# Down weights of the experts issued from ScalarE's queue behind its eviction of the results, gate and up weights left on SyncE's queue

## The reference, cut to what matters

```python
def hier_moe(x, w_group, w_expert, w_gate, w_up, w_down):
    ...
    hid = jax.nn.silu(lax.ragged_dot(xs, w_gate, sizes)) * lax.ragged_dot(xs, w_up, sizes)
    ys = lax.ragged_dot(hid, w_down, sizes) * weight.reshape(-1)[order][:, None].astype(x.dtype)
    return jax.ops.segment_sum(ys, tok_sorted, num_segments=n_tok).reshape(b, s, d)
```

## Time and profile before

| | us |
|---|---|
| median of 3 runs | 3278.77 (3275.36 to 3280.22) |
| the profiled execution | 3283.96 |
| its span, first to last instruction | 3282.1 |
| first expert stage, first gate matmul to last down matmul | 331.0 to 816.4 |
| second expert stage, the same | 1242.6 to 1728.0 |

### The profile page before, as it was taken

How to read it: one execution, slowest core, us unless ns; L and a number is a source line. 1 busy time by engine, 2 the same in 40 slices (tenths; PEclk the granted TensorE clock), 3 DMA queues, 4 the chain that set the end, 5 groups by cost and what they waited for, 6 DMA issues and landing times. The chain is left out here.

```text
span 3282.1 us, 37064 instructions
## 1 busy us (share of the span) xinstructions
PE 2668.1 (81%) x13270; PEld 1813.9 (55%) x13270; DVE 1187.2 (36%) x2020; ACT 789.8 (24%) x1304; POOL 225.7 (7%) x313
## 2 busy tenths in 40 slices
PE   8885998877488868988882986799996987599997
PEld 4534665444234445654441763577785763477776
DVE  2544110000345441100005745455533744455532
ACT  0320010000035300100001225244421325244421
POOL 0001111111000001111110000000001000000000
PEclk9997999999699978999996998899998999799999
DMA  3043999998410348999993300222222210222221
GB/s 119 1 188 136 365 406 409 409 406 331 133 26 1 143 180 322 403 408 409 411 372 113 103 26 13 90 90 89 89 90 70 93 39 13 77 90 89 89 90 64
DMA packets 189581, 573.97 MB, mean 175 GB/s; under 512 B 40656, under 2 KB 119952, under 8 KB 140082
## 3 DMA queue, kind: packets, MB, share of 16 engines
q1 hardware_dynamic: 178930, 555.97, 44.5%
q0 software_dynamic: 10560, 16.81, 1.6%
HBM read 567.47 MB, written 23.07 MB: 180 GB/s over the span
## 5 line engine op out<-in xcount | busy, mean ns | idle before, releaser
L1281 PE MATMUL ps<-layer_h_hi,layer_w_hi 128*128 128x512 f32 x1024 | 406.2, 397 | 49.2 <-issue 23.6
L1283 PE MATMUL ps<-layer_h_hi,layer_w_lo 128*128 128x512 f32 x1024 | 399.8, 390 | 0.0
L1282 PE MATMUL ps<-layer_h_lo,layer_w_hi 128*128 128x512 f32 x1024 | 399.3, 390 | 0.0
L859 PE MATMUL ps<-w_weights,moe_xsT 128*64 128x256 f32 x2688 | 313.8, 381 | 55.6 <-DMA w_weights<-in_moe_w_up 35.3
L914 DVE TENSOR_TENSOR moe_hid<-moe_silu,ps 128x256 f32<-128x256 f32 x64 | 27.0, 421 | 796.7 <-PE ps L859 796.7
L859 PEld LDWEIGHTS ps<-w_weights,moe_xsT 128*64 128x64 f32 x2688 | 223.2, 137 | 155.9 <-issue 107.1
L1281 PEld LDWEIGHTS ps<-layer_h_hi,layer_w_hi 128*128 128x128 f32 x1024 | 192.6, 188 | 112.3 <-issue 70.1
L1332 DVE TENSOR_TENSOR layer_w_lo<-layer_raw,layer_w_hi 128x2048 fp32r<-128x2048 f32 x52 | 119.2, 2292 | 279.7 <-ACT layer_w_hi L1328 279.7
L1283 PEld LDWEIGHTS ps<-layer_h_hi,layer_w_lo 128*128 128x128 f32 x1024 | 192.6, 188 | 41.2
L1282 PEld LDWEIGHTS ps<-layer_h_lo,layer_w_hi 128*128 128x128 f32 x1024 | 192.8, 188 | 38.9 <-issue 0.8
L877 PE MATMUL ps<-w_weights,moe_hidT 128*64 128x512 f32 x672 | 180.6, 685 | 38.5 <-DVE moe_hidT L916 38.5
(11 more groups left out here) (350 smaller groups left out, 3853.2 us busy)
## 6 DMA issues: line engine op xcount, KB each, us to landing
w_weights<-in_moe_w_gate SPq DMA_DIRECT2D x84, 1024.0 KB, 28.2
w_weights<-in_moe_w_up SPq DMA_DIRECT2D x84, 1024.0 KB, 29.1
w_weights<-in_moe_w_down SPq DMA_DIRECT2D x84, 1024.0 KB, 28.9
first_ring<-in_moe_w_gate SPq DMA_DIRECT2D x44, 1024.0 KB, 28.2
first_ring<-in_moe_w_up SPq DMA_DIRECT2D x44, 1024.0 KB, 29.1
first_ring<-in_moe_w_down SPq DMA_DIRECT2D x44, 1024.0 KB, 29.0
layer_raw<-in_ffn_up SPq DMA_DIRECT2D x44, 1024.0 KB, 5.1
layer_raw<-in_w_in SPq DMA_DIRECT2D x24, 1024.0 KB, 5.1
```

The source lines that it names most:

```text
L859: ins = pe.matmul(k.ps[64 * h:64 * h + 64, 2 + m, 0:256], xsT[:, j, :], weights.gate_up[s][m][:, j, 256 * h:256 * h + 256], start=j == 0, ...
L1281: pe.matmul(out, stationary[0], moving[0], start=first, stop=False)
L1282: pe.matmul(out, stationary[0], moving[1], start=False, stop=False)
L1283: return pe.matmul(out, stationary[1], moving[0], start=False, stop=last)
```

## The change

SyncE no longer issues the down weights in the loops over the first 31 blocks. ScalarE does: after it has copied the result of block b to `ys`, it issues the two down chunks of expert b+3, with no wait of their own, because it has already waited for `used[s][5]`. The gate and up weights stay on SyncE's queue, and so do all six chunks of the first three experts and of the last loop.

```diff
-    def load(self, sp, s, e, before):
+    def load(self, sp, s, e, before, with_down=True):
...
+        if with_down:
+            self.load_down(sp, s, e, before)
+
+    def load_down(self, eng, s, e, before):
+
+        a = self.k.a
         for c in range(2):
             before(4 + c)
-            sp.dma_start(self.down[s][:, 2 * c:2 * c + 2, :].rearrange("p j c -> p (j c)"),
+            eng.dma_start(self.down[s][:, 2 * c:2 * c + 2, :].rearrange("p j c -> p (j c)"),
                          a["moe_w_down"][self.layer, e, c * 256:(c + 1) * 256, :].rearrange("(p j) c -> p (j c)", j=2)).then_inc(self.loaded[s][4 + c], 16)
...
             with sp.Fori(1, TURNS) as i:
                 for s in range(WEIGHT_SETS):
-                    weights.load(sp, s, i * WEIGHT_SETS + s, free(s, i))
+                    weights.load(sp, s, i * WEIGHT_SETS + s, free(s, i), with_down=False)
             for s in range(LAST_SET):
-                weights.load(sp, s, TURNS * WEIGHT_SETS + s, free(s, TURNS))
+                weights.load(sp, s, TURNS * WEIGHT_SETS + s, free(s, TURNS), with_down=False)
...
-            for_each_block(act, n, body)
+            def body_and_load(s, times, b):
+                body(s, times, b)
+                weights.load_down(act, s, b + WEIGHT_SETS, lambda c: None)
+
+            with act.Fori(0, TURNS - 1) as i:
+                for s in range(WEIGHT_SETS):
+                    body_and_load(s, i, i * WEIGHT_SETS + s)
+            for s in range(WEIGHT_SETS):
+                (body_and_load if s < LAST_SET else body)(s, TURNS - 1, (TURNS - 1) * WEIGHT_SETS + s)
+            for s in range(LAST_SET):
+                body(s, TURNS, TURNS * WEIGHT_SETS + s)
+            with act.Fori(0, n) as q:
+                body(LAST_SET, q + TURNS, q + (EXPERTS - 1))
```

## The result

The changed kernel takes 3294.85 us (median of 5 runs, 3289.14 to 3296.95), the kernel before 3275.97 beside it (5 runs, 3274.73 to 3280.22). The ratio is 1.0053, 95% interval 1.0038 to 1.0067: 12 to 22 us slower, about 17 (the two medians are 18.9 us apart). The forecast was +9. The time lies inside the wide range, 3273 to 3304, that had to cover the rivals too; it lies just above the 3281 to 3294 of the forecast itself, and +17 is above the +3 to +14 of its mechanism. The profiled execution has a span of 3295.1 us, 13.0 more than before.

What follows compares the result with a forecast made beforehand. DMA transfers of weights were taken to bound the expert stages. Zero terms plus tail growth of 3.7 and 5.2 us gave 8.9, taken as 9: 3278.77 + 9 = 3287.8 us; forecast's own range 3281 to 3294, wide range 3273 to 3304.

Steps and rivals of the forecast that it cites:

- Issue time: On SyncE: taking two load issues of six from it gains nothing, 0 us.
- ScalarE's hold: On ScalarE: two more issues behind each copy, about 0.9 us, fit in before silu is needed, 0 us.
- start of the loads: Down loads issued after the copy start slightly later; DMA engines still have queued work, 0 us.
- The order in which chunks are served: DMA queues take turns; down chunks overtake gate and up chunks, landing in about 9.8 us; the part with a price.
- T: Landing of a stage's last weight chunk, set by the sum of transfers; expected within 2 us of 811.8 in the first stage.
- Gate loads "still some 28" us: Sign expected in the profile: gate loads on SyncE's queue still land some 28 us after issue.
- The tail, +3.7 and +5.2: TensorE's end behind the last landing grows to 8.3 us, by 3.7 in the first expert stage and 5.2 in the second.
- so block 30 starts at T - 19.2: Stage end: block 29's last up chunk lands at T - 27.2, and block 30's first matmul follows 8.0 us later.
- Nothing moves: Rival: second queue served behind the first, or TensorE's lead at the end as before; -3 to +3 us, chance 0.20.
- Starvation: Rival: ScalarE's queue gets under a third of the turns, down chunks come late; 3306 us, chance 0.06.
- Disturbance: Rival: two queues slow each other's transfers, up to 210 us (3490); any size above 0.1 us per block, chance 0.07.
- Faster: Rival: three queues taking turns halve the gather's collision cost, 22 us off and 9 added; 3266 us, chance 0.11.

Runs made afterwards that it cites:

- run after the next silu: Changed kernel, but ScalarE issues the two down loads behind the next block's silu instead of behind the copy: 3296.57 us, ratio 1.0051 to the kernel before.
- run with one row: Kernel before, with ScalarE issuing two extra loads of one 16-byte row per block into an unused tile: 3281.25 us, ratio 1.0011.
- one chunk: Changed kernel, but ScalarE issues only chunk 5 of each expert and chunk 4 stays on SyncE: 3283.3 us, ratio 1.0018 to the kernel before.
- every second: Kernel before, with ScalarE issuing chunks 1, 3 and 5 of experts 3 to 30 and SyncE chunks 0, 2 and 4: 3282.11 us, ratio 1.0019.
- halved kernel before: Kernel before with half of the gate and up matmuls left out, all loads and copies kept: 3268.93 us, ratio 0.9977 to the full kernel before.

## Why the prediction was right, and where it was off

*Issue time 0, ScalarE's hold 0, start of the loads 0*: right. ScalarE's timeline around a pair of issues:

```profile
594.14 0.60 ACT L901 ACTIVATE moe_ys<-ps 128x512 f32<-128x512 f32 x1 [9.24 <-PE ps L883]
594.30 0.83 ACTq L756 DMA_DIRECT2D w_weights<-in_moe_w_down  x2
595.45 1.28 ACT L898 ACT_TABLE_LOAD   x1 [0.71 <-issue]
597.53 0.38 ACT L898 ACTIVATE moe_silu<-ps 128x256 f32<-128x256 f32 x1 [0.80 <-PE ps L865]
```

The pair takes 0.83 us, and silu still waits 0.80 us for TensorE behind the table.

*The order in which chunks are served*: right in kind, too short in time. Down loads land 9.7 us (first) and 14.5 us (second) after issue; 9.7 us is four times 2.46, the time that I gave to the pair, but only the first chunk has landed by then: the pair takes half as long again as I had it. Each queue does get about half the turns (the 1.52 and 1.51 MB above), but not from the start: in the first 5 us after an issue ScalarE's queue moves 0.39 MB and SyncE's 1.45. First waits come at block 10, before block 15. The copies to `ys` come every 16.0 us in the middle:

```profile
L901 ACT ACTIVATE moe_ys<-ps x20: 597/597/597, 488.4 to 792.2; 128x512 f32<-128x512 f32 x20
```

(792.2 - 488.4)/19 = 15.99 us, with blocks 28 to 29 already at TensorE's pace. T is later by 1.1 and 0.7 us, within the 2 us allowed, and the last three blocks wait for nothing.

*Gate loads "still some 28" us*: wrong, in the second execution of the changed kernel, where the trace pairs them, they take 33 to 47, with a median of 41. SyncE is still held (a median of 1.9 us for a gate issue in the middle of the first stage, as before), so I take its queue to hold as many chunks as before, some eleven; in the middle of the stage it has only four sixths of the transfers, and 28.2 x 6/4 = 42 us. It changed nothing in the sum, because the count at the end goes by the order of landing and not by latency.

*The tail, +3.7 and +5.2*: the mechanism was right and the term too small; it measured +6.8 per stage. The count back from T was good: block 29's last up chunk landed at 782.07, T - 27.4 (predicted T - 27.2). The step that failed is the one that follows, "so block 30 starts at T - 19.2": block 30 no longer started from that landing. TensorE was at its own pace from block 29 on, one block earlier. Block 28's last up chunk landed at 767.54, T - 41.9, and from there to block 29's first matmul it took 778.88 - 767.54 = 11.3 us, not the 8.0 of the earlier trace rows. After the wait of 2.77 us the up matmuls took 3.60 instead of 1.95 us and the down matmuls 5.35 instead of 3.65: 3.35 us, all of the difference. The granted clock says why: it is at the lower level from 767.6 to 771.1 us and again from 774.5 to 777.9, and at the upper level between and behind. The last stretches of the changed kernel:

```profile
741.00:779.00 38.00, 32.37 (x197) 18.80 (x195) 2.88 (x6) 1.96 (x4) 4.95 (x10) 0.87 1.02 404
779.00:792.00 13.00, 12.06 (x94) 8.10 (x92) 1.44 (x3) 0.98 (x2) 2.37 (x4) 1.00 1.01 407
```

and the same part of the stage before:

```profile
741.00:783.00 42.00, 33.00 (x228) 19.98 (x229) 4.33 (x9) 2.31 (x5) 6.09 (x11) 1.00 1.02 409
```

Matmuls at 3.60 us where 1.95 is usual run at the lower level, 1.2 GHz. The other three stages of the changed kernel show the same: the last wait for weights, 2.4 to 2.8 us long, comes in block 27 or 28, matmuls behind it run at the lower level, and no later block waits. I had taken each distance from stretches in which waits are short (1.14 us) and evenly spread, and so missed that the waits come in lumps and that the clock falls behind a long one, at just that place. From T - 30.6, three blocks at TensorE's pace (41.0 us) give T + 10.4, as measured; with 8.0 us instead of 11.3, block 30 would have set T + 8.3 as predicted.

The run after the next silu comes near it in its average, 8.35, but that is the mean of 7.0 and 9.7; in its first stage block 30 starts at T - 19.2, as predicted, and then two blocks at 13.0 us follow instead of two of 13.67. The term for T, put at 0, was 0.9 us per stage. So the sum was 8.9 us where the profiles show 15.5, and that the time fell inside the stated range is owed to the width that the rivals gave it.

*The rivals.* Nothing moves: no, the tails moved. Starvation: no, ScalarE's queue has half the turns. Disturbance: at most small; T is later by 0.9 us per stage, some 2 us per kernel rather than 210. Faster: no; T did not come earlier. The Trainium skill (DMA: Bandwidth & Descriptors, "Queues, rings and completion order") has each DMA engine go round its queues a packet at a time, and the landings agree. The same page's "Issuing engines are not separate DMA queues" says that a second issuing engine saves only issue time; here it saved none, and the kernel got 0.5% slower, mostly through the order of service.

What stays open: how much of the 17 us is the second queue's own cost. The tails and T leave 2 us of it, the run with one row says 1 to 7, and every full kernel with loads on ScalarE's queue up to the last blocks cost at least 0.11%, also those whose tails are the ones of before (one chunk 0.18%, every second 0.19%, one row 0.11%). What makes up those small costs was not separated.

## What to carry to other kernels

Moving part of a full stream of loads to another engine's queue does not only save issue time, it lets that part overtake. Where the transfers set the pace, look at which chunk lands last and how much work still hangs on it: what overtakes should be what is needed first, and the last blocks of a stage should keep the order of need (here, putting experts 24 to 30 back on one queue removed the whole cost). Count such a tail back from the last landing to the first block that no longer waits, and take the distances from places with the same clock.

## What the runs showed of the hardware that I had not expected

- The granted clock depends on how the waits are spread, and not on their sum alone. With nearly the same sum in a stage (33.3 to 41.2 us in the changed kernel, 36.6 to 43.3 before) but half as many waits, the changed kernel has 0.88 to 0.94 instead of 0.96 to 0.99 in the second part of the stage. The sum matters too: in the halved kernel before, with 66 waits for weights of at most 2.1 us but 79.5 us in all, the clock stays low block after block; the stretch of its blocks 27 to 29 reads:

```profile
728.00:779.00 51.00, 39.45 (x180) 17.75 (x178) 4.33 (x9) 4.22 (x7) 7.14 (x12) 0.70 1.02 403
```

- Loads of 128 rows of 16 bytes are dear beside a full stream: 0.24 MB took 0.3% of all 16 engines' time, and T moved by 4 us per stage.
- SyncE was held no less with four chunks per expert in its queue than with six: a gate issue's median in the middle of a stage is 1.9 to 3.1 us in the four stages of the changed kernel, 1.9 in those before. With every second chunk on ScalarE's queue it was hardly held: the median of its issues is 0.33 us.
- The 16 DMA engines are not in step. One 1 MB chunk of the changed kernel had its first recorded sixteenth landed at 590.3 and its last at 603.4 us. Before the change the spread in the middle of the first stage is 4 to 13 us, with a median of 7.6.
